# Final norm of a decoder trunk: the multiply by the norm weights moved to Pool, the scaling to ScalarE

## The reference

```
def rmsnorm(x, g):
    xf = x.astype(F32)
    y = xf * lax.rsqrt(jnp.mean(xf * xf, axis=-1, keepdims=True) + RMS_EPS)
    return (y * g.astype(F32)).astype(x.dtype)
...
    y_prompt = rmsnorm(xp, norm_final)
    y_sample = rmsnorm(xs, norm_final)
```

## Time and profile before

| | us |
|---|---|
| Median of 3 runs | 1405.23 |
| Lowest and highest of them | 1402.44, 1411.34 |
| The profiled execution, its device time | 1403.18 |
| Its span in the trace | 1401.2 |

### The profile page before, as it was taken

One profiled execution on the slowest core, in us unless ns is written; L12 is line 12 of the kernel. 1 busy time (PEld: TensorE's weight loads), 2 busy tenths in 40 slices (PEclk: granted clock), 3 DMA queues, 4 the chain that ended last, 5 costly groups with the idle time before them and its releaser, 6 DMA issues.

```text
span 1401.2 us, 16227 instructions
## 1 busy us (share of the span) xinstructions
PE 1232.1 (88%) x6277; PEld 653.9 (47%) x6277; DVE 370.7 (26%) x793; ACT 246.6 (18%) x572; POOL 214.5 (15%) x268
## 2 busy tenths in 40 slices
PE   7999998889899899788867999999799899888880
PEld 5764575556644533333324764445564533333330
DVE  4231003544411611111115400111630532111115
ACT  2000004653302100000003200012520301000011
POOL 2300002322100011111001000211940011111102
PEclk9999999999999999989998999999999999999995
DMA  8310504859967689999958132212149679999965
GB/s 287 103 47 22 190 5 133 269 179 346 365 247 318 237 331 420 419 420 419 412 217 291 33 103 50 80 55 69 46 151 364 247 254 416 419 420 420 418 271 210
DMA packets 103677, 339.97 MB, mean 243 GB/s; under 512 B 21454, under 2 KB 40082, under 8 KB 79786
## 3 DMA queue, kind: packets, MB, share of 16 engines
q1 hardware_dynamic: 88456, 302.84, 56.9%
q0 software_dynamic: 14848, 35.94, 7.1%
q10 hardware_dynamic: 290, 0.07, 0.0%
HBM read 322.18 MB, written 31.31 MB: 252 GB/s over the span
## 4 chain that ended last, share of the span: by engine, by line
PE 52%; SPq 22%; DMA 8%; DVE 7%; issue 4%; POOL 3%; ACT 2%; POOLq 2%; PEldq 1%; PEld 0%; DVEq 0%; ACTq 0%
SPq L1116 11%; PE ps L1838 8%; SPq L1138 6%; PE ps L1326 6%; PE ps L1251 6%; PE ps L468 4%; PE ps L446 4%; PE ps L1789 4%; SPq L1124 3%; DMA moe_wd<-in_moe_w_down 3%; PE ps L1344 3%; DMA fox_arena<-negs_rows 2%; PE ps L361 2%; PE ps L758 1%; PE ps L776 1%
## 5 line engine op out<-in xcount | busy, mean ns | idle before, releaser
L1326 PE MATMUL ps<-moe_gu,rows 128*64 128x512 f32 x1024 | 247.1, 638 | 54.1 <-DMA moe_gu<-in_moe_w_up 50.9
L1326 PEld LDWEIGHTS ps<-moe_gu,rows 128*64 128x64 f32 x1024 | 82.2, 146 | 198.7 <-issue 190.0
L1613 DVE TENSOR_TENSOR turned<-turned,ps 128x256 f32<-128x256 f32 x32 | 13.5, 421 | 305.4 <-ACT turned L1429 305.4
L1210 POOL DMA_INDIRECT expert_rows<-turned,moe_row x32 | 32.1, 1004 | 392.0 <-ACT turned L1439 359.4
L1344 PE MATMUL ps<-moe_wd,moe_rowsel 128*64 128x512 f32 x352 | 80.4, 598 | 2.9 <-DMA moe_wd<-in_moe_w_down 2.9
L1429 ACT ACTIVATE turned<-ps 128x256 f32<-128x256 f32 x32 | 12.3, 384 | 303.1 <-PE ps L1326 303.1
L468 PE MATMUL ps<-turned,fox_arena 128*128 128x288 f32 x256 | 62.3, 406 | 0.0
L446 PE MATMUL ps<-fox_arena,turned 128*128 128x512 f32 x128 | 56.0, 593 | 2.9 <-issue 2.9
L1838 PE MATMUL ps<-mwblk,turned 128*128 128x512 f32 x128 | 56.0, 594 | 1.5 <-DVE vaug L2041 1.5
L1838 PE MATMUL ps<-m_arena,turned 128*128 128x512 f32 x128 | 55.7, 593 | 0.7 <-ACT m_arena L1928 0.7
L361 PE MATMUL ps<-turned,fox_arena 128*128 128x288 f32 x224 | 55.2, 406 | 0.0
(11 more groups left out here) (365 smaller groups left out, 1689.8 us busy)
## 6 DMA issues: line engine op xcount, KB each, us to landing
moe_gu<-in_moe_w_gate SPq DMA_DIRECT2D x56, 1024.0 KB, 21.7
moe_gu<-in_moe_w_up SPq DMA_DIRECT2D x56, 1024.0 KB, 23.5
moe_wd<-in_moe_w_down SPq DMA_DIRECT2D x44, 1024.0 KB, 24.7
rows<-in_moe_w_down SPq DMA_DIRECT2D x20, 1024.0 KB, 22.8
fox_arena<-in_cache_v POOLq DMA_DIRECT2D x32, 512.0 KB, 10.3
fox_arena<-in_fox_w_in SPq DMA_DIRECT2D x6, 2048.0 KB, 10.2
fox_arena<-in_cache_k SPq DMA_DIRECT2D x20, 512.0 KB, 8.3
moe_gu<-in_moe_w_gate SPq DMA_DIRECT2D x16, 512.0 KB, 10.8
```

Of the source, the lines that this page charges most:

```text
L1326: mm = pe.matmul(ps[h, 2 + p % 2, :].rearrange("s (k f) -> s k f", k=2), xT[:, c, h], gu[s][:, half, :, c, :], start=(c == 0), stop=(c == ...
```

## The change

Pool gets a multiply of each full tile by the norm weights, `weighed = x * gl` (128x1024), issued once the tile's second add is done and ahead of the tile's power in Pool's stream. ScalarE then scales `weighed` by `rstd` into `rows`, behind the square of the next tile. VectorE keeps adds and means; the single product remains on it for the sample tile alone, with a semaphore of its own. A tensor of 4 tiles (16 KB a partition) is added for `weighed`, and two semaphores.

```diff
             sb("f_held", [P, KC + 2 * NT + 1, D], where=fin)
+            weighed = sb("f_weighed", [P, NT - 1, D], where=fin)
+            weighted, last_ended = sem("f_weighted"), sem("f_last_ended")
...
             def sp_(sp):
                 for n in range(NT):
-                    sp.wait_ge(ended, n + 1)
+                    if n < L:
+                        sp.wait_ge(ended, n + 1)
+                    else:
+                        sp.wait_ge(last_ended, 1)
...
             def pool_(pool):
+                pool.wait_ge(gl_in, 16)
                 for n in range(NT):
+                    if n < L:
+                        pool.wait_ge(combined, 2 * n + 2)
+                        pool.tensor_tensor(weighed[:, n, :], x[:, n, :], gl, ALU.mult).then_inc(weighted, 1)
                     pool.wait_ge(meaned, n + 1)
                     pool.tensor_tensor(rstd[:, n:n + 1], ms[:, n:n + 1], const("minus_half")[:, 0:1], ALU.pow).then_inc(rooted, 1)
...
                     act.activation(rows[0:r, n, :], x[0:r, n, :], ACT.Square, accum_out=sq[0:r, n:n + 1]).then_inc(squared, 1)
+                    if n:
+                        scale(act, n - 1)
+
+            def scale(act, n):
+
+                act.wait_ge(weighted, n + 1)
+                act.wait_ge(rooted, n + 1)
+                act.activation(rows[:, n, :], weighed[:, n, :], ACT.Copy, scale=rstd[:, n:n + 1]).then_inc(ended, 1)
...
                 dve.scalar_tensor_tensor(rows[0:r, n, :], x[0:r, n, :], rstd[0:r, n:n + 1], gl[0:r, :], ALU.mult, ALU.mult
-                                         ).then_inc(ended, 1)
+                                         ).then_inc(last_ended, 1)
...
                     combine(dve, 1, n, 1, combined)
-                    if n:
-                        end(dve, n - 1)
                 mean(dve, L)
                 end(dve, L)
```

## The result

The changed kernel takes 1408.66 us, the kernel before 1404.61 in the same comparison (medians of 20 runs each): a ratio of 1.0028, 95% interval 1.0016 to 1.0040, so 3.9 us more (2.2 to 5.6); the medians themselves are 4.05 apart. Forecast were 1407.5 us, +2.3. The profiled execution took 1404.43 us at a span of 1402.4.

What follows compares the result with a forecast made beforehand. Untouched phases fill most of the span; the last is a ring of VectorE's adds and product and Pool's power. 1.94 + 0.82 - 0.42 = +2.3 us on 1405.23 gives 1407.5 us, range 1402.4 to 1411.5.

Steps and rivals of the forecast that it cites:

- The price of the multiply: Pool's new 128x1024 multiply: 2.33 us by the slope of two shorter instructions, with 1.90 and 2.92 as ends.
- Who waits for whom: Pool's multiply and VectorE's adds take turns: multiply ends 2.18 us behind the add, a waiting add 1.13 behind the multiply.
- no-hold-up rival: Last phase: Pool multiplies beside VectorE's adds without blocking them, -5.3 us; chance 0.12.
- Pool keeps its turn through multiply and power: Last phase: Pool holds VectorE's second add out until the power ends, together +4.6 us; chance 0.10.
- First blocked add: Second add of tile 1 waits for tile 0's multiply, ending at 1383.36 instead of 1381.42: +1.94 us, paid once.
- three periods: Three tile periods of add, multiply and add, 4.51 us each: 13.53 in place of 12.71, +0.82 us.
- tail: End of the last add to issue of the samples' store: 3.31 us instead of 3.73, -0.42.
- the stage: Start of the last phase's first add to issue of the samples' store; 21.61 us in the kernel before.
- rows 6: Profile rows of VectorE's L2048 meeting Pool's L2100: each waits; the released one ends its duration less 0.15 us later.
- The power: Pool's 128x1 power waits for VectorE's add but holds nobody, cost nothing; rival that it holds VectorE: +3.2 us, chance 0.10.
- rows 7: Profile rows of a power issued under an add, ending at 742.84; the next add from 742.45 still takes 1.28 us.
- a power gets its turn between two back-to-back adds: Last phase: otherwise it waits one add more, +2.6 us with another timeline; chance 0.60 covers either turn.

Runs made afterwards that it cites:

- the half multiply: Changed kernel with Pool multiplying 512 of 1024 columns, result unread, and ScalarE scaling x itself: last phase to the samples' store 19.56 us, 4.28 less than the change.
- the multiplies behind everything: Changed kernel with Pool's four multiplies after its five powers and ScalarE's scalings after its five squares: last phase to the samples' store 26.84 us.
- the kernel with the later product: Kernel before with VectorE's product issued one add later, nothing moved to another engine: ratio to before 0.9977, last phase to the samples' store 19.84 us.
- the kernel with the multiply on VectorE: Changed kernel with the multiply by weights on VectorE instead of Pool, ScalarE still scaling: ratios to before 0.9972 and 0.9991, last phase to samples' store 19.43 us.
- two further comparisons: Changed kernel run twice more, unedited, against the kernel before: ratios 1.0002 and 1.0011, last phase to the samples' store 23.84 and 23.91 us.
- a second power: Changed kernel with each full tile's power done twice, first into a spare tensor: last phase to the samples' store 24.83 us.
- the four-piece kernel: Changed kernel with Pool's multiply cut into four instructions of 256 columns: last phase to the samples' store 25.13 us, 1.3 above the change.

## Why the prediction was right, and where it was off

**The price of the multiply.** 2.33 us forecast from two shorter instructions, 2.33 to 2.34 measured alone. The two shorter ones were adds of a mask, one of them on 64 partitions only; that neither matters here was an assumption that came out. The row of the same size, 1.90, was the wrong guide, as one of its inputs repeats an element. Two additions of one shape in the kernel before show what that does: 1.263 us at 64x512 with a full row (L1763), 1.035 with a repeated element (L1766). The second of them, from the trace of the kernel before (ns min/median/max):

```profile
L1766 POOL TENSOR_TENSOR mws<-mws,nat x1: 1035/1035/1035, 894.3 to 894.3; 64x512 f32<-64x512 f32 x1
```

**Who waits for whom.** Right. The multiply ends 2.20 behind the add (2.18 forecast), the add 1.08 behind the multiply (1.13), recorded with 3.19 (3.2 forecast). One meeting of two instructions in another phase carried this. The no-hold-up rival, at -5.3 us, is what the same rows without the turns would have given; the half multiply and the multiplies behind everything exclude it. The rival in which Pool keeps its turn through multiply and power falls too: the power is issued at 1381.17, before the multiply ends at 1381.21, and the waiting add still ends 1.08 behind the multiply, ahead of the power.

**The sum.** First blocked add +1.91 (1.94), three periods +0.73 (0.82, the period 4.48 instead of 4.51), tail -0.41 (-0.42): +2.23 in the stage against +2.3. What was a little off is what a released add still takes: it ends its own 1.28 less 0.20 behind the multiply, where the prediction took 0.15 off, as in rows 6.

**The power.** It holds nobody, as rows 7 had it: the add behind it keeps 1.27. On this point the page "SBUF — State Buffer" of the Trainium skill, whose section "🔬 SBUF: two separate sides" has the pair locked for the whole instruction, was set against the row, and the row decided. For the multiply the trace agrees but for the last 0.14 to 0.20 us: the loser ends 2.20 (multiply) or 1.08 us (add) behind the other's end, somewhat less than its own 2.34 or 1.28. That a power gets its turn between two back-to-back adds was left open in the prediction; it does, here and in the kernel with the later product.

**ScalarE and the stores.** The scalings cost nothing, as forecast; the kernel with the multiply on VectorE shows it. Off was that the stores would move by one to two us: the last tile's is issued 22.8 us into the stage (1397.97 - 1375.21), about 3.1 us later than before (1395.87 - 1376.25 = 19.6), and the first 2.4 us later (1384.53 - 1375.21 against 1383.18 - 1376.25). It is still 1.1 us ahead of the samples' and hides.

**The whole time.** 1408.66 us measured, 1407.5 forecast. That these are only 1.2 us apart is in part luck: the base, a median of three runs, was 0.6 us too high (1405.23 against 1404.61 over twenty), and the forecast effect 1.75 us below the 4.05 by which the medians differ. The measured difference of 3.9 us is larger than the stage's 2.23, which lies at the low end of its interval; two further comparisons gave 0.3 and 1.5 us. I take the rest for scatter from one set of runs to the next, because it did not come again and the stage did; that is argued, not shown. The longer executions have the lower granted clock of TensorE; what moves it in the untouched phases was not tried.

**In the experiments** the step that failed was the price of a second power, set at its length alone. Under VectorE's adds a 128x1 power takes the rest of the add and 0.4 us more (1.54 and 1.19 us recorded), not its own 0.54.

## What to carry to other kernels

Work moved from VectorE to Pool need not be off VectorE's path. Here, where both sides read two large tensors from SBUF, the 1.28 us product became a 2.34 us multiply during which VectorE's adds stood still; no run tried one input or an operand elsewhere than in SBUF, so which property of the two instructions decides was not shown. Before such a move, look in the trace for instructions recorded longer than their twins; that is where an engine is blocked without an idle time to show it. If a product waits for a small result, try to split it so that the large part needs no wait, or to issue it one instruction later: both kept the multiply by the weights on VectorE and took 2.2 and 1.8 us off this phase.

## What was not expected of the hardware

Turns, which the kernel before showed in one meeting, are strict also between full queues: in the first stretch of the four-piece kernel a 128x256 piece of Pool's and a 128x1024 add of VectorE's alternate with no gap in either queue, ending 0.59 and 1.08 us behind each other. And a 128x1 power, which takes 0.54 us alone, waits for its turn like a large instruction and ends 0.42 us after it, yet leaves the add that starts beside it at 1.27 us.
